# Two sums moved ahead of an addition, and a looser wait for their transfers, in a Strassen MLP

## The chip, the cores and the metric

The kernel runs on one core of one Trainium2 chip. The metric is device time in microseconds, 1420.25 us for the kernel before (median of 3 runs, 1419.57 to 1420.36). A core has TensorE for matrix products, VectorE, ScalarE and GpSimd for elementwise work, and SyncE, which here only issues transfers. Each engine works through its own list of instructions in order; they meet at semaphores. TensorE writes to eight banks of PSUM, everything else lives in SBUF.

## The reference

Two transformer blocks in float32 on 512 tokens of width 1024 (the second with 16 more). The attention parts are of no matter here. Each block ends in an MLP with a squared ReLU:

```
x = x + jnp.square(jax.nn.relu(h2 @ w_mlp_in[layer])) @ w_mlp_out[layer]      # first block
hdn = jnp.square(jax.nn.relu(jnp.einsum('bld,df->blf', u, w_ff1)))            # second block
return jnp.einsum('blf,fd->bld', hdn, w_ff2)
```

The hidden width is 4096.

## The kernel before

Every float32 product is made of three: each operand is split into a high part (the float32 rounded to the matmul's own format, written by ScalarE) and a low part (the rest, a subtraction on VectorE), and TensorE adds high x high, high x low and low x high in PSUM. So every weight passes ScalarE and then VectorE before TensorE may use it.

An MLP takes its hidden width in four chunks of 1024. The first three of each MLP run in a hardware loop over `strassen_chunk`, six chunks in all; the fourth is dense. In a chunk, eight slabs (j = 0 to 7) make the hidden values with dense products at L2120. The second matrix is then applied in four column pairs (q = 0 to 3) of 256 output columns, each as a 2 x 2 block product in the Strassen-Winograd form, with 7 products (128 output columns, 512 of k, 256 tokens) instead of 8. One such product is `block_product` at L2168: 4 blocks of k times 3 matmuls of 256 columns, 12 in all, so 84 a pair and 336 a chunk. Its order in a pair is A11 B11, S1 T1, S2 T2, S3 T3, S4 B22, A12 B21, A22 T4. S1 to S4 are sums of quarters of the weights, T1 to T4 differences of quarters of the hidden values.

Who makes what:

- S1 and S3 come from transfers that GpSimd issues in `s13_sums`: first two plain ones (the base, L738), and when these have landed two that accumulate onto them (L741). There are two buffers, pair q and pair q+2 share one.
- S2 and S4 are VectorE's `second_sum` (L1390: S1 plus a quarter of the weights that SyncE loaded) and `fourth_sum` (L1396). ScalarE writes their high parts (L896, in pair 0 L888 and L892), VectorE the low ones: `last_low` (L1418), and for pair 0 `second_low` (L1410) and `fourth_low` (L1414). S4's low part gives the semaphore s4_lo.
- `upper_left` (L1400) and `first_sums` (L1405) are the low parts of A11 and of S1 with S3; `lower` (L1423) those of A12 and A22.
- PSUM is used in two sets of four banks, one for odd and one for even pairs. In a pair the partial sums of two banks are needed in `mids` as well as in the output. VectorE adds them there twice: `first_mids` (L1432) after the first two products, and L1494 after S2 and S3. Both give mid_read. TensorE waits for the first before S4 B22 and for the second before A22 T4, since those products go on adding in banks that VectorE has to read first.
- At the end of a pair VectorE adds to X at L1503 and L1507.
- For the last hidden slab (j = 7) the differences T2 and T4 are still being split while pair 0 runs: L1473 is the low part of T2, L1478 that of T4. TensorE waits for them by k, through `ready` and `all_ready`.

The order on every engine is the order in which this code is written; no scheduler changes it.

Of the kernel before, what the change touches and what calls it, by code (L numbers as in the profile page):

```python
# [47 lines left out]
B11, T1, T2_, T3, T4, B21, B22 = range(7)  # L48
# [123 lines left out]
def build(nc, d):  # L172
# [21 lines left out]
    with ctx:  # L194
# [165 lines left out]
        s2_hi, s2_lo, s4_hi, s4_lo = sem("s2_hi"), sem("s2_lo"), sem("s4_hi"), sem("s4_lo")  # L360
# [299 lines left out]
        def _(pool):  # L660
# [64 lines left out]
            def s13_sums(which, c, q):  # L725
# [7 lines left out]
                if u > 1:  # L733
                    pool.wait_ge(s13_lo, u - 1)
                    pool.wait_ge(s2_sum, u - 1)
                for o, s in ((0, S3), (1, S1_)):
# [565 lines left out]
        def _(dve):  # L1302
# [69 lines left out]
            def strassen_chunk(which, c):  # L1372
# [62 lines left out]
                for j in range(8):  # L1435
# [24 lines left out]
                    else:  # L1460
# [7 lines left out]
                        if j == 6:  # L1468
                            upper_left(0)
                        if j == 7:  # L1470
                            first_mids(0)
                        dve.wait_ge(hid_hi, parts + 4 + 2 * k + 1)
                        dve.tensor_tensor(hidden_part(Hl, k, T2_, 2), h[:, 0:2].rearrange("p b n -> p (b n)"),  # L1473
                                          hidden_part(Hh, k, T2_, 2), ALU.subtract).then_inc(hid_lo, 1)
                        if j == 7:
                            fourth_low(0)
                        dve.wait_ge(hid_hi, parts + 4 + 2 * k + 2)
                        dve.tensor_tensor(hidden_part(Hl, k, T4, 3), h[:, 2:5].rearrange("p b n -> p (b n)"),  # L1478
# [6 lines left out]
                for q in range(4):  # L1485
# [4 lines left out]
                    if q > 0:  # L1490
                        first_mids(q)
                    dve.wait_ge(blk_done, done + 4)
                    dve.wait_ge(mid_read, reads + 2 * q + 1)
                    dve.tensor_tensor(mid, mid, ps[:, g2:g4 + 1, 0:HB], ALU.add).then_inc(mid_read, 1)  # L1494
                    if last:
                        slab_weights(p0, 0, t + 17)
                    else:
                        upper_left(q + 1)
                        second_sum(q + 1)
                        fourth_sum(q + 1)  # L1500
                        first_sums(q + 1)
# [601 lines left out]
        def _(pe):  # L2103
# [49 lines left out]
            def strassen_chunk(which, c):  # L2153
# [8 lines left out]

                def block_product(a, b, bank, first, ready=None, ks=range(4)):
                    for k in ks:
                        if ready is not None:
# [11 lines left out]
                for q in range(4):  # L2177
# [18 lines left out]
                    else:  # L2196
                        pe.wait_ge(s4_lo, pairs + q + 1)
                    block_product(S2_, T2_, g2, True, ready, range(3))
                    block_product(S3_, T3, g4, True, None, range(3))
                    block_product(S2_, T2_, g2, True, ready, range(3, 4)).then_inc(blk_done, 1)  # L2200
                    block_product(S3_, T3, g4, True, None, range(3, 4)).then_inc(blk_done, 1)
                    pe.wait_ge(s4_lo, pairs + q + 1)
# [500 lines left out]
```

## Time and profile before

| what | value |
|---|---|
| median of 3 runs | 1420.25 us |
| the profiled execution's own time | 1420.25 us |
| its span | 1418.5 us |
| TensorE busy | 1410.9 us, 99% |
| VectorE busy | 898.3 us, 63% |
| ScalarE busy | 578.8 us, 41% |
| GpSimd busy | 197.6 us, 14% |
| share of the chain of waits at the dense products, L2120 | 65% |
| share at the block products, L2168 | 17% |

The span runs from the first to the last instruction that the profile holds; the time of the execution has 1.75 us more around it. A busy share tells how full an engine is, not what an instruction waits for; for that the views by wait and by time are needed. "PE" is TensorE's matmuls and "PEld" its weight loads, which overlap them; DVE is VectorE, ACT ScalarE, POOL GpSimd, SP SyncE.

### The profile page before, as it was taken

The numbers are of one execution on the slowest core, as the hardware profiler recorded it, in microseconds if no ns is written. First come the engines' busy times: TensorE is split into PE (matmuls) and PEld (weight loads), VectorE is DVE, ScalarE is ACT, GpSimd is POOL, SyncE is SP. The second block draws the span as 40 slices with busy tenths as digits, with TensorE's granted clock in tenths as the row PEclk, the third lists the DMA queues.
The fourth block names the chain that finished last, engine by engine and source line by source line (L and its number), as shares of the span: only waits on it lengthen the run. The fifth ranks groups of instructions, "written<-read, shape, count | busy, mean of one in ns | idle before, by whom it ended". The sixth has DMA issues, their size and how long they took to land.

```text
span 1418.5 us, 21381 instructions
## 1 busy us (share of the span) xinstructions
PE 1410.9 (99%) x8574; PEld 1183.2 (83%) x8574; DVE 898.3 (63%) x1200; ACT 578.8 (41%) x828; POOL 197.6 (14%) x204
## 2 busy tenths in 40 slices
PE   9999999999999999999999999999999999999998
PEld 7887778777888989989878997778888998989886
DVE  5535433665757858577656778656756858668652
ACT  4124531554445435353244435343344535344232
POOL 4000000000022302211322020000022211302300
PEclk9999999999999999999999999999999999999999
DMA  5223113201236745635323222232236663836321
GB/s 182 89 90 111 61 61 108 70 30 60 98 108 164 183 131 147 159 109 148 102 77 104 90 68 76 83 99 74 92 105 157 160 166 101 202 111 178 109 84 60
DMA packets 154715, 156.35 MB, mean 110 GB/s; under 512 B 3866, under 2 KB 148612, under 8 KB 154644
## 3 DMA queue, kind: packets, MB, share of 16 engines
q1 hardware_dynamic: 125444, 130.16, 28.8%
q0 software_dynamic: 29184, 25.17, 10.0%
q8 instruction: 52, 0.85, 0.3%
q14 instruction: 19, 0.16, 0.0%
q10 hardware_dynamic: 16, 0.00, 0.0%
HBM read 152.44 MB, written 2.10 MB: 109 GB/s over the span
## 4 chain that ended last, share of the span: by engine, by line
PE 98%; DVE 1%; ACT 1%; issue 0%; POOL 0%; POOLq 0%; DVEq 0%
PE ps L2120 65%; PE ps L2168 17%; PE ps L2116 4%; PE ps L2237 3%; PE ps L2466 1%; PE ps L2493 1%; PE ps L2479 1%; PE ps L2582 1%; DVE wl L1313 1%; PE ps L2285 0%; PE ps L2370 0%; PE ps L2277 0%; PE ps L2346 0%; PE ps L2411 0%; PE ps L2390 0%; PE ps L2262 0%
## 5 line engine op out<-in xcount | busy, mean ns | idle before, releaser
L2120 PE MATMUL ps<-AA,wh 128*128 128x512 f32 x1600 | 505.3, 397 | 0.4
L2120 PEld LDWEIGHTS ps<-AA,wh 128*128 128x128 f32 x1600 | 296.7, 188 | 71.8 <-DVE wl L1313 2.9
L2120 PE MATMUL ps<-BB,wh 128*128 128x512 f32 x1088 | 342.5, 396 | 0.2 <-issue 0.2
L2120 PE MATMUL ps<-AA,wl 128*128 128x512 f32 x800 | 314.9, 394 | 0.0
L2120 PEld LDWEIGHTS ps<-BB,wh 128*128 128x128 f32 x1088 | 202.2, 188 | 49.7 <-issue 1.9
L829 ACT ACTIVATE wh<-raw 128x1024 fp32r<-128x1024 f32 (+2 forms) x149 | 141.5, 950 | 233.4 <-PE ps L2120 222.4
L2120 PE MATMUL ps<-BB,wl 128*128 128x512 f32 x544 | 213.9, 393 | 0.0
L1313 DVE TENSOR_TENSOR wl<-raw,wh 128x1024 fp32r<-128x1024 f32 (+2 forms) x149 | 174.9, 1174 | 49.4 <-ACT wh L829 49.0
L2120 PEld LDWEIGHTS ps<-AA,wl 128*128 128x128 f32 x800 | 150.5, 188 | 34.2
L2120 PEld LDWEIGHTS ps<-BB,wl 128*128 128x128 f32 x544 | 102.3, 188 | 23.2
L2168 PE MATMUL ps<-Hl,wh 128*128 128x256 f32 x384 | 108.7, 283 | 0.0
L1349 DVE TENSOR_TENSOR arena<-ps,RS 128x512 f32<-128x512 f32 (+2 forms) x59 | 40.8, 691 | 88.2 <-PE ps L2120 82.9
L2168 PE MATMUL ps<-Hl,Sh 128*128 128x256 f32 x288 | 80.9, 281 | 0.0
L1381 DVE TENSOR_TENSOR wl<-raw,wh 128x1024 fp32r<-128x1024 f32 x48 | 62.3, 1297 | 28.8 <-ACT wh L875 13.7
L2168 PEld LDWEIGHTS ps<-Hl,wh 128*128 128x128 f32 x384 | 73.3, 191 | 0.0
L875 ACT ACTIVATE wh<-raw 128x1024 fp32r<-128x1024 f32 x36 | 38.3, 1063 | 70.3 <-PE ps L2120 70.1
L1443 DVE SCALAR_TENSOR_TENSOR zf<-ps,RS 128x512 f32<-128x512 f32 x48 | 33.2, 691 | 47.8 <-PE ps L2120 47.2
L2168 PEld LDWEIGHTS ps<-Hl,Sh 128*128 128x128 f32 x288 | 54.6, 190 | 0.3
L2168 PE MATMUL ps<-AA,wh 128*128 128x256 f32 x192 | 54.2, 282 | 0.0
L2168 PE MATMUL ps<-BB,wh 128*128 128x256 f32 x192 | 54.2, 282 | 0.0
L2168 PE MATMUL ps<-AA,wl 128*128 128x256 f32 x192 | 53.7, 280 | 0.0
L2168 PE MATMUL ps<-BB,wl 128*128 128x256 f32 x192 | 53.7, 280 | 0.0
(331 smaller groups left out, 2185.2 us busy)
## 6 DMA issues: line engine op xcount, KB each, us to landing
raw<-in_w_in SPq DMA_DIRECT2D x38, 1024.0 KB, 5.5
raw<-in_w_ff SPq DMA_DIRECT2D x29, 1024.0 KB, 5.5
raw<-in_w_mlp_in SPq DMA_DIRECT2D x16, 1024.0 KB, 5.4
raw<-in_w_mlp_out SPq DMA_DIRECT2D x16, 1024.0 KB, 5.3
zf<-in_w_mlp_out POOLq DMA_DIRECT2D x48, 256.0 KB, 4.4
zf<-in_w_ff POOLq DMA_DIRECT2D x48, 256.0 KB, 4.3
raw<-in_w_out SPq DMA_DIRECT2D x8, 1024.0 KB, 5.2
late<-in_w_ff SPq DMA_DIRECT2D x3, 1024.0 KB, 5.4
```

The costliest lines, as they stand in the source:

```text
L829: act.activation(w_slab(wh, t % 2, kt), raw_slab(t), ACT.Copy).then_inc(hi_ready, 1)
L875: act.activation(w_slab(wh, j % 2, KT), raw_half((p0 + i) % 2, j % 2, KT, 2), ACT.Copy)\
L1313: dve.tensor_tensor(w_slab(wl, t % 2, kt), raw_slab(t), w_slab(wh, t % 2, kt), ALU.subtract)\
L1349: dve.tensor_tensor(tokens(dst, kind), dense_psum(t, kind)[0:rows], tokens(scale, kind), ALU.mult)\
L1381: dve.tensor_tensor(w_slab(wl, slot, KT), raw_half(p % 2, slot, KT, 2), w_slab(wh, slot, KT), ALU.subtract).then_inc(lo_ready, 1)
L1443: dve.scalar_tensor_tensor(out=f, in0=halves(dense_psum(t0 + j, which)), scalar=0.0, in1=halves(RS[:, 0:S1]), op0=ALU.max, op1=ALU.mult).t ...
L2116: last = pe.matmul(dense_psum(t_ps, ALL)[:, half, :], a[:, k, :], b[:, o0 + k, half * HALF2:(half + 1) * HALF2], start=start, stop=stop)
L2120: last = pe.matmul(dense_psum(t_ps, kind), a[:, k, :], b[:, o0 + k, col0:col0 + S1], start=start, stop=stop)
L2168: mm = pe.matmul(ps[:, bank, 0:HB], w[:, k, :], hidden_part(x, k, b), start=(first and k == 0 and i == 0), stop=(k == 3 and i == 2), skip_ ...
L2237: mm = pe.matmul(out, x[:, k, tok], w[:, k, cols], start=False, stop=(k == KT - 1 and i == 2), skip_group_check=True)
L2466: pe.matmul(ps[:, 2 + b, 0:nk], qb[rows, hp, n * P:(n + 1) * P], kb[rows, hp, 0:nk], start=True, stop=False)
L2479: mm = pe.transpose(ps[:, 4 + b, i * P:(i + 1) * P], pair(Sg[w % 2], nk)[:, b, i * P:(i + 1) * P], ident[:, :])
```

## The change

There are three edits, all in the Strassen chunks. GpSimd's transfers for the sums of pair q wait for s4_lo of pair q-2 in place of two other semaphores of that pair. VectorE runs `first_mids(0)` behind `fourth_low(0)`, and `second_sum(q + 1)` and `fourth_sum(q + 1)` ahead of the second addition to `mids` in pair q. TensorE runs all of S2 T2 and then all of S3 T3, where before their fourth k came behind the first three of both.

```diff
--- before.py
+++ after.py
@@ -731,8 +731,7 @@
                 if c == 0 and q == 0:
                     pool.wait_ge(slab_done, MLPS[which][0] + 1)
                 if u > 1:
-                    pool.wait_ge(s13_lo, u - 1)
-                    pool.wait_ge(s2_sum, u - 1)
+                    pool.wait_ge(s4_lo, u - 1)
                 for o, s in ((0, S3), (1, S1_)):
                     at = slice(q * 256 + o * P, q * 256 + o * P + P)
                     pool.dma_start(blk(sums[:, s]), rows[0:S1, at].rearrange("(k p) n -> p k n", p=P))                        .then_inc(s13_base, 16)
@@ -1467,13 +1466,12 @@
                                                  op0=ALU.mult, op1=ALU.subtract).then_inc(t4_diff, 1)
                         if j == 6:
                             upper_left(0)
-                        if j == 7:
-                            first_mids(0)
                         dve.wait_ge(hid_hi, parts + 4 + 2 * k + 1)
                         dve.tensor_tensor(hidden_part(Hl, k, T2_, 2), h[:, 0:2].rearrange("p b n -> p (b n)"),
                                           hidden_part(Hh, k, T2_, 2), ALU.subtract).then_inc(hid_lo, 1)
                         if j == 7:
                             fourth_low(0)
+                            first_mids(0)
                         dve.wait_ge(hid_hi, parts + 4 + 2 * k + 2)
                         dve.tensor_tensor(hidden_part(Hl, k, T4, 3), h[:, 2:5].rearrange("p b n -> p (b n)"),
                                           hidden_part(Hh, k, T4, 3), ALU.subtract).then_inc(hid_lo, 1)
@@ -1489,6 +1487,9 @@
                     mid = halves(mids[:, q])
                     if q > 0:
                         first_mids(q)
+                    if not last:
+                        second_sum(q + 1)
+                        fourth_sum(q + 1)
                     dve.wait_ge(blk_done, done + 4)
                     dve.wait_ge(mid_read, reads + 2 * q + 1)
                     dve.tensor_tensor(mid, mid, ps[:, g2:g4 + 1, 0:HB], ALU.add).then_inc(mid_read, 1)
@@ -1496,8 +1497,6 @@
                         slab_weights(p0, 0, t + 17)
                     else:
                         upper_left(q + 1)
-                        second_sum(q + 1)
-                        fourth_sum(q + 1)
                         first_sums(q + 1)
                     dve.wait_ge(blk_done, done + 6)
                     dve.tensor_tensor(halves(x0), halves(x0), ps[:, g1:g3 + 1, 0:HB], ALU.add)
@@ -2160,8 +2159,8 @@
                 S4_, S2_ = (blk(wh[:, 0, upper]), blk(wl[:, 0, upper])), (blk(wh[:, 0, lower]), blk(wl[:, 0, lower]))
                 A11_, S3_, S1_ = ((blk(Sh[:, i * S1:(i + 1) * S1]), blk(Sl[:, i * S1:(i + 1) * S1])) for i in range(3))
 
-                def block_product(a, b, bank, first, ready=None, ks=range(4)):
-                    for k in ks:
+                def block_product(a, b, bank, first, ready=None):
+                    for k in range(4):
                         if ready is not None:
                             ready(k)
                         for i, (w, x) in enumerate(((a[0], Hh), (a[0], Hl), (a[1], Hh))):
@@ -2195,10 +2194,8 @@
                             pe.wait_ge(hid_lo, parts + 4 + 2 * k + 2)
                     else:
                         pe.wait_ge(s4_lo, pairs + q + 1)
-                    block_product(S2_, T2_, g2, True, ready, range(3))
-                    block_product(S3_, T3, g4, True, None, range(3))
-                    block_product(S2_, T2_, g2, True, ready, range(3, 4)).then_inc(blk_done, 1)
-                    block_product(S3_, T3, g4, True, None, range(3, 4)).then_inc(blk_done, 1)
+                    block_product(S2_, T2_, g2, True, ready).then_inc(blk_done, 1)
+                    block_product(S3_, T3, g4, True).then_inc(blk_done, 1)
                     pe.wait_ge(s4_lo, pairs + q + 1)
                     pe.wait_ge(mid_read, reads + 2 * q + 1)
                     block_product(S4_, B22, g3, False, all_ready).then_inc(blk_done, 1)
```

What this moves on TensorE, in pair 0 of a chunk. Weights in `wh` and `wl` are S2's, those in `Sh` and `Sl` are S3's; the wait for hid_lo is for one k of T2's low part. Before, from the third k of S3 to its fourth, with the fourth k of S2 between them:

```order
L2168 MATMUL ps<-AA,Sh 128x256
L2168 MATMUL ps<-Hl,Sh 128x256
L2168 MATMUL ps<-AA,Sl 128x256
L2193 REGISTER_ALU
L2168 MATMUL ps<-AA,wh 128x256 [waits hid_lo]
L2168 MATMUL ps<-Hl,wh 128x256
L2168 MATMUL ps<-AA,wl 128x256
L2168 MATMUL ps<-AA,Sh 128x256
L2168 MATMUL ps<-Hl,Sh 128x256
L2168 MATMUL ps<-AA,Sl 128x256
```

and now the third and the fourth k of S2, with S3 from there on:

```order
L2167 MATMUL ps<-AA,wh 128x256 [waits hid_lo]
L2167 MATMUL ps<-Hl,wh 128x256
L2167 MATMUL ps<-AA,wl 128x256
L2192 REGISTER_ALU
L2167 MATMUL ps<-AA,wh 128x256 [waits hid_lo]
L2167 MATMUL ps<-Hl,wh 128x256
L2167 MATMUL ps<-AA,wl 128x256
L2167 MATMUL ps<-AA,Sh 128x256
L2167 MATMUL ps<-Hl,Sh 128x256
L2167 MATMUL ps<-AA,Sl 128x256
L2167 MATMUL ps<-AA,Sh 128x256
```

The wait for the fourth k of T2's low part comes nine matmuls earlier, and the matmuls are the same.

On VectorE in pair 0, from `first_mids(0)` (L1432) to `upper_left(1)` (L1400), before:

```order
L1432 TENSOR_TENSOR zf<-zf,ps 128x512
L1472 REGISTER_ALU
L1473 TENSOR_TENSOR Hl<-zf,AA 128x512
L1414 TENSOR_TENSOR wl<-zf,wh 128x512
L1477 REGISTER_ALU
L1478 TENSOR_TENSOR Hl<-zf,AA 128x768
L1422 REGISTER_ALU
L1423 TENSOR_TENSOR wl<-raw,wh 128x1024
L1492 REGISTER_ALU
L1494 TENSOR_TENSOR zf<-zf,ps 128x512
L1399 REGISTER_ALU
L1400 TENSOR_TENSOR Sl<-raw,Sh 128x512
```

and now, from `fourth_low(0)` (L1413) to the second addition to `mids` (L1495); the low part of T2 (L1470) stands directly ahead of the first row. Line numbers are those of the changed kernel:

```order
L1413 TENSOR_TENSOR wl<-zf,wh 128x512
L1430 ISA
L1431 TENSOR_TENSOR zf<-zf,ps 128x512
L1475 REGISTER_ALU
L1476 TENSOR_TENSOR Hl<-zf,AA 128x768
L1421 REGISTER_ALU
L1422 TENSOR_TENSOR wl<-raw,wh 128x1024
L1389 TENSOR_TENSOR zf<-zf,raw 128x512
L1394 REGISTER_ALU
L1395 TENSOR_TENSOR zf<-raw,zf 128x512
L1493 REGISTER_ALU
L1495 TENSOR_TENSOR zf<-zf,ps 128x512
```

`first_mids(0)` (now L1431) has moved behind the low parts of T2 and S4, and the two sums (now L1389 and L1395) stand ahead of the second addition, where before they came behind it and behind `upper_left(1)`.

On GpSimd, the transfers of pair 2 of the first chunk and the beginning of pair 3, before:

```order
L738 DMA zf<-in_w_mlp_out 128x4x128 [waits s2_sum,s13_lo]
L738 DMA zf<-in_w_mlp_out 128x4x128
L741 DMA zf<-in_w_mlp_out 128x4x128 [waits s13_base]
L741 DMA zf<-in_w_mlp_out 128x4x128
L738 DMA zf<-in_w_mlp_out 128x4x128 [waits s2_sum,s13_lo]
```

and now:

```order
L737 DMA zf<-in_w_mlp_out 128x4x128 [waits s4_lo]
L737 DMA zf<-in_w_mlp_out 128x4x128
L740 DMA zf<-in_w_mlp_out 128x4x128 [waits s13_base]
L740 DMA zf<-in_w_mlp_out 128x4x128
L737 DMA zf<-in_w_mlp_out 128x4x128 [waits s4_lo]
```

The transfers stand where they stood; only what the first of each pair waits for has changed.

## Rows read from the trace of the kernel before

**Rows 1.** Busy time of the engines, and the granted clock by slice, from the page.
```profile
PE 1410.9 (99%) x8574; PEld 1183.2 (83%) x8574; DVE 898.3 (63%) x1200; ACT 578.8 (41%) x828; POOL 197.6 (14%) x204
...
PEclk9999999999999999999999999999999999999999
```

**Rows 2.** Chain of waits in order of time: start us, us, engine, line, count.
```profile
462.27 39.90 PE ps L2168 x336
502.17 44.48 PE ps L2120 x192
```

**Rows 3.** Waits: engine and line <- releaser: us in total, times, longest us.
```profile
PE ps L2277 <- POOL ident L671: 1.7, 1, 1.7
...
DVE zf L1494 <- PE ps L2168: 33.9, 18, 2.1
```

**Rows 4.** Timeline: start us, us, engine, line, operation; TensorE in pair 0.
```profile
465.87 0.19 PEld L2168 LDWEIGHTS ps<-AA,Sh 128*128 128x128 f32 x1
...
470.53 0.19 PEld L2168 LDWEIGHTS ps<-AA,wh 128*128 128x128 f32 x1
470.64 0.28 PE L2168 MATMUL ps<-AA,wh 128*128 128x256 f32 x1
```

**Rows 5.** Timeline, VectorE in pair 0.
```profile
465.13 0.69 DVE L1432 TENSOR_TENSOR zf<-zf,ps 128x512 f32<-128x512 f32 x1 [0.21 <-PE ps L2168]
465.74 0.68 DVE L1473 TENSOR_TENSOR Hl<-zf,AA 128x512 fp32r<-128x512 f32 x1
...
467.81 1.22 DVE L1423 TENSOR_TENSOR wl<-raw,wh 128x1024 fp32r<-128x1024 f32 x1
468.94 0.68 DVE L1494 TENSOR_TENSOR zf<-zf,ps 128x512 f32<-128x512 f32 x1
...
470.14 0.69 DVE L1390 TENSOR_TENSOR zf<-zf,raw 128x512 f32<-128x512 f32 x1
470.94 0.69 DVE L1396 TENSOR_TENSOR zf<-raw,zf 128x512 f32<-128x512 f32 x1
471.54 1.22 DVE L1405 TENSOR_TENSOR Sl<-zf,Sh 128x1024 fp32r<-128x1024 f32 x1
...
473.28 1.22 DVE L1418 TENSOR_TENSOR wl<-zf,wh 128x1024 fp32r<-128x1024 f32 x1
```

**Rows 6.** Timeline, ScalarE in pair 0.
```profile
464.50 0.63 ACT L920 ACTIVATE AA<-zf 128x512 fp32r<-128x512 f32 x1 [0.83 <-DVE zf L1464]
465.03 0.62 ACT L892 ACTIVATE wh<-zf 128x512 fp32r<-128x512 f32 x1
```

**Rows 7.** Timeline, a stall of TensorE on a dense slab of the second block.
```profile
741.70 2.03 DVE L1313 TENSOR_TENSOR wl<-raw,wh 128x1024 fp32r<-128x1024 f32 x1 [0.20 <-ACT wh L829]
...
743.79 0.30 PEld L2120 LDWEIGHTS ps<-AA,wh 128*128 128x128 f32 x2 [0.58 <-DVE wl L1313]
...
744.12 0.19 PEld L2120 LDWEIGHTS ps<-AA,wl 128*128 128x128 f32 x1
```

**Rows 8.** Timeline, VectorE in pair 1.
```profile
477.94 0.69 DVE L1494 TENSOR_TENSOR zf<-zf,ps 128x512 f32<-128x512 f32 x1 [1.37 <-PE ps L2168]
```

**Rows 9.** Timeline, transfers issued by GpSimd for the sums, and one by SyncE.
```profile
430.30 2.60 POOL L738 DMA_DIRECT2D zf<-in_w_mlp_out  x2
440.32 2.63 POOL L741 DMA_DIRECT2D zf<-in_w_mlp_out  x2 [7.42 <-DMA zf<-in_w_mlp_out]
457.74 1.54 POOL L738 DMA_DIRECT2D zf<-in_w_mlp_out  x2 [14.79 <-DVE zf L1390]
...
469.19 0.37 SPq L609 DMA_DIRECT2D raw<-in_w_mlp_out  x1
...
473.06 1.55 POOL L738 DMA_DIRECT2D zf<-in_w_mlp_out  x2 [8.18 <-DVE Sl L1405]
477.77 2.62 POOL L741 DMA_DIRECT2D zf<-in_w_mlp_out  x2 [3.17 <-DMA zf<-in_w_mlp_out]
```

**Rows 10.** DMA issues of 478.77 to 479.37: kind, KB each, us to landing.
```profile
zf<-in_w_mlp_out POOLq DMA_DIRECT2D x2, 256.0 KB, 5.8
```

## The prediction

> **What bounds the kernel now.** I read the page first. TensorE is busy 1410.9 of 1418.5 us [rows 1], so a change can gain only where TensorE waits, and costs only where it makes TensorE wait. The chain of waits then shows where the changed code stands: the four column pairs of one chunk are one unbroken piece of 336 matmuls in 39.90 us [rows 2], and there are six such pieces (three chunks in each of two MLPs). That is 0.1188 us a matmul and 9.97 us a pair. The list of waits has TensorE wait 1.7 us once, at the start of the program, and nowhere at the line of the block products [rows 3]. So nothing in the changed stretch can be won by taking a wait away. The question is whether the new order brings a producer behind TensorE. For that I lay the timeline of TensorE beside those of VectorE, ScalarE and GpSimd in the first of the six pieces and compare each semaphore that TensorE waits for with the time at which TensorE gets there. The other five pieces repeat it.
>
> TensorE's marks in pair 0 [rows 4]: the 34th of its 84 weight loads at 465.87; the last product (A22, the 73rd to 84th matmul) loads weights at 470.53 and multiplies from 470.64. Counted on from there, pair 1 starts at 470.64 + 12 x 0.1188 = 472.07, and its own A22 at 470.64 + 9.97 = 480.61.
>
> **The change part by part.**
>
> *Order of the products S2 and S3 on TensorE.* The same 24 matmuls are issued, twelve and twelve instead of 9, 9, 3, 3. The last of them ends at the same place, and nobody waits for the signal of S2 alone. The piece runs at one pitch, switches of product included, so I cost the order itself at 0 (bound: the last rival, 0.03 us a switch). What moves is one wait: in pair 0 the fourth k of S2 needs the low part of T2_ (VectorE L1473), and now needs it at the 34th weight load, 465.87, instead of nine matmuls later (466.94). In its old place, at 465.74 behind `first_mids` [rows 5], L1473 would be late by 0.5 us. In the new order it comes ahead of `first_mids` and waits only for ScalarE's L920, which ends at 464.50 + 0.63 = 465.13 [rows 6]. A waiting engine starts about 0.06 us after its releaser's end [rows 7], so L1473 runs about from 465.18 to 465.87: a tie. If it is lost, it costs 0.0 to 0.1 us, and it does not add to what follows, since the term below is set by VectorE alone.
>
> *`first_mids(0)` behind `fourth_low(0)`.* From L1432 to L1494 VectorE runs without a gap, 465.13 to 468.94 = 3.81 us [rows 5]. It is the same five instructions in another order, all their inputs are there (ScalarE's L892 for `fourth_low` ends at 465.65 [rows 6]). The run starts at 465.18, so the first instruction behind it starts at 468.99. `first_mids` itself ends 1.2 us later than before, at 467.06 by three instructions of 0.60 us; TensorE's S4 product wants it 24 loads ahead of 470.53, at about 467.7. Hidden, with 0.6 us in hand.
>
> *`second_sum(q+1)` and `fourth_sum(q+1)` ahead of the second addition to `mids`.* This is the term that I think decides. TensorE may not start A22 of pair q, which goes on writing the same bank, until the second addition to `mids` (L1494) has read it. Before, in pair 0, L1494 ran 468.94 to 469.62, 0.9 us before TensorE's weight load at 470.53 [rows 4, 5]. Now two sums stand ahead of it. Their pitches are read from the same place: L1390 at 470.14, L1396 at 470.94, the next at 471.54, that is 0.80 + 0.60 = 1.40 us [rows 5]. So L1494 starts at 468.99 + 1.40 = 470.39 and ends at 470.39 + 0.68 = 471.07. TensorE needed it 0.5 us earlier.
>
> What such a wait costs is seen at a stall on a dense slab. VectorE ends at 741.70 + 2.03 = 743.73, the weight load starts at 743.79 and the third one at 744.12 [rows 7]. In a running stream a load starts with the matmul ahead of its own, and the pitch there is 44.48 / 192 = 0.23 us [rows 2]; so the third load marks the second matmul, and the first ran from 743.89, 0.16 us after VectorE's end. Here that gives 471.07 + 0.16 = 471.23 against 470.64: **0.59 us lost in pair 0 of each chunk**. Behind it TensorE is again the only bound, so it stays lost: 6 x 0.59 = 3.5 us.
>
> The cover in the other pairs: in pair 1 VectorE stood idle 1.37 us, until the S3 product was done, before L1494 at 477.94 [rows 8], so from 476.57. The two sums fill that gap, and L1494 has until about 479.8. In the pairs behind it the gap is up to 2.1 us [rows 3]. Hidden, as long as the sums' data have landed. The rest of VectorE's order in pair 0 ends where it ended: L1405 started at 471.54, and now at 468.99 + 1.40 + 0.60 + 0.60 = 471.59; L1418 behind it ends at 474.55 (before 474.50) for a wait of TensorE 24 matmuls into pair 1, at about 474.8, which itself moves 0.59 us later. L1400, now behind L1494, ends at 470.39 + 0.60 + 0.69 = 471.68 for the first product of pair 1 at 472.07 + 0.59. Each of these is hidden.
>
> *GpSimd's wait.* The transfers that build the sums of pair q+2 now start behind the low part of S4 of pair q instead of behind the second sum and the low parts of S1 and S3. For pair 2 this is a delay from 457.74 [rows 9] to about 466.8: `fourth_low(0)` ends at 465.18 + 0.60 + 0.69 = 466.47, and GpSimd issued 0.30 us after its releaser's end at 473.06 (471.54 + 1.22 = 472.76) [rows 5, 9]. From there the fitting row is the transfers of pair 3, which also share the DMA engines with a 1 MB load of SyncE: 473.06 to 477.77 for the base, 1.3 us to the second accumulating issue, 5.8 us to its landing [rows 9, 10], 11.8 us in all. So pair 2's sums land at 466.77 + 11.84 = 478.6, and `second_sum(2)` starts at 478.7. VectorE then stands 2.1 us on this wait (from 476.57), with L1494 queued behind it. L1494 then ends at 478.67 + 1.40 + 0.68 = 480.75, and A22 of pair 1 starts at 480.91 instead of 480.61: 0.3 us late. But pair 0 has already put TensorE back by 0.59, so this second lateness lies inside the first and adds nothing: per chunk the larger of the two counts. It starts to add when `second_sum(2)` begins after 478.96. Bounds: at the least the transfers cost nothing (with `second_sum(2)` at 478.37 they would be in time even alone). At the most they take what pair 1's took in the first chunk, 430.30 to 440.32 for the base alone [rows 9], 5.3 us more: a loss of 5.6 us in pair 1 instead of 0.59 in pair 0, 34 us in all. I take the 11.8 us, because that slow case was issued right behind the accumulating transfers of pair 0, while at 466.8 GpSimd's queue has long been empty. Pair 3's transfers now start behind L1418 at about 474.9 (before 473.06) and land at 486.7; TensorE needs them by about 488.9. Those of the next chunk's pairs 0 and 1 start 0.5 to 2 us later than before with over 20 us in hand.
>
> A rule of the skill speaks the other way. The Trainium skill ("DMA: Bandwidth & Descriptors", section "Anatomy of one DMA — SWDGE (gpsimd) path") fits a GpSimd-issued transfer as 2.0 us plus its bytes at 436 GB/s, 2.6 us for 256 KB. By it the sums would land at about 474.1 and GpSimd's wait would cost nothing at all. This case's trace does not agree for accumulating transfers, 5.8 us [rows 10], so the trace decides; the forecast is the same by either.
>
> **Sum.** Added 6 x 0.59 = 3.5 us; removed 0. The profiled execution took 1420.25 us, 1.75 around its span of 1418.5, and that is also the median of the runs. Forecast 1423.8 us, +0.25%. A measurement of this kernel tells about 0.2% (2.8 us) from no change.
>
> **Rivals.**
>
> *The weights are already in.* If the blocked product's weight load need not wait, the first matmul starts at 471.07 + 0.06 and the loss is 0.49 us, 2.9 us in all: 1423.2. For it: loads run 0.11 us ahead of their matmuls here [rows 4]. Against it: the one stall that is seen has its load behind the wait [rows 7], though there it waited for the weights themselves. The Trainium skill ("TensorE: Matmul & The Clock Gate", step "LDWEIGHTS — get the stationary operand into the array") says that the queue pulls weight loads ahead of matmuls in flight; by that rule the time would be this one. No row here shows it across a wait.
>
> *TensorE catches up.* The pitch of 118.8 ns for 256 columns [rows 2] is 0.464 ns a column, that of 231.7 ns for 512 columns 0.453, at the upper of the clock's two levels throughout [rows 1]; so at least 2.9 ns of a block product's matmul is not columns. If that surplus is issue time, the queue fills during a stall, and the 264 matmuls from there to the end of the piece could give 0.59 us back: 1420.3, no slower than before. It decides from 2.2 ns of recovery a matmul. Against it: the 192 matmuls of a dense stretch and the 336 of a piece each keep one pitch [rows 2], with SyncE, VectorE and ScalarE coming and going beside them, and no stretch is seen to run faster. Likewise, if L1494's read came in time after all, the time would be this one.
>
> *The sums land late.* Pair 2's transfers start 2.4 us before SyncE's load at 469.19 [rows 9], and pair 3's meet theirs at another point, so the sharing may be worse. At 1 us later than I say, `second_sum(2)` begins at 479.7, pair 1 loses 1.3 us instead of 0.59, and the kernel 7.8 us: 1428.
>
> *The new order itself is faster.* Two switches of product fewer per pair; at 0.03 us each, 48 of them give 1.4 us, with no stall 1418.8. No pitch in the trace shows such a cost.
>
> **How the numbers follow.** Forecast (0.59 us a chunk) 0.58; weights already in 0.12; catching up or in time 0.13; late sums 0.14; faster order 0.03. The likeliest one's own range is 1423.0 to 1424.6. The range of 8 in 10 leaves out the catching up below and the worse half of the late sums: 1421.5 to 1427.0. Faster by over 0.2%: 0.03. Within 0.2%: the catching up, a third of the case with weights in, and a few hundredths of the forecast's lower edge, 0.20. Slower: 0.77.
>
> **What would show it.** Right: the waits list a new one of TensorE at the block products for L1494 (now L1495), six times, near 0.5 us each; each piece of 336 matmuls takes 40.5 us instead of 39.90; VectorE waits for a DMA ahead of `second_sum(2)` and GpSimd's wait there names L1413. The forecast is wrong if pair 0 shows no gap at A22, if the gap stands at pair 1 and exceeds 0.6 us (late sums), or if the pieces still take 39.9 us.

## The result, and the profile after

| | us, median (lowest to highest, runs) | ratio to before, 95% interval |
|---|---|---|
| before | 1420.25 (1419.57 to 1420.41, 5) | |
| changed | 1428.4 (1424.97 to 1431.81, 5) | 1.0061 [1.0041, 1.0082] |

The kernel became slower, by 8 us, where I forecast 3.5 us. The time of 1428.4 us lies outside my range of 1421.5 to 1427.0. It also spreads over 7 us from run to run, where the kernel before kept within 0.9. The profiled execution of the changed kernel took 1423.29 us (span 1421.6), less than all five timed ones, so its trace shows the fixed part of the loss well and the rest only at its smallest.

The chain of waits after (start us, us, engine and line, count) answers to [rows 2]. Line 2119 is the dense products and 2167 the block products.

```profile
420.09 41.72 PE ps L2119 x180
...
470.56 31.38 PE ps L2167 x264
501.94 44.49 PE ps L2119 x192
...
1302.06 0.78 POOL zf L740
1302.84 7.05 DMA zf<-in_w_ff
1310.01 0.70 DVE zf L1389
1311.34 0.69 DVE zf L1495
1312.08 11.58 PE ps L2167 x96
1323.66 44.49 PE ps L2119 x192
```

The first piece began at 420.09 + 41.72 = 461.81 and ended at 501.94: 40.13 us instead of 39.90. It is no longer one link: the chain enters it at 470.56, the A22 product of pair 0. The last piece is entered much later, at 1312.08, by way of a transfer that took 7.05 us. The six pieces took 40.13, 40.22, 40.13, 40.69, 40.12 and 41.49 us.

The waits (engine and line <- releaser: us in total, times, longest us) answer to [rows 3]. L1495 is the second addition to `mids`, L1389 `second_sum`, L1413 the low part of S4, L737 GpSimd's base transfers.

```profile
DVE zf L1389 <- DMA zf<-in_w_ff: 12.7, 6, 3.9
DVE zf L1495 <- PE ps L2167: 12.4, 6, 2.2
DVE zf L1389 <- DMA zf<-in_w_mlp_out: 12.0, 6, 2.6
...
PE ps L2167 <- DVE zf L1495: 2.6, 8, 1.1
```

Three of these are new. VectorE waits for a DMA ahead of `second_sum` twelve times: six are pair 2, as forecast, and six are pair 3, which I had in time. TensorE waits for L1495 eight times, not six: in pair 0 of each chunk, once in pair 1 (0.36 us, in the fourth chunk) and once in pair 2 (1.28 us, in the sixth).

Pair 0 on VectorE and TensorE (timeline: start us, us, engine, line, operation) answers to [rows 4, 5]; this execution runs 0.47 us ahead of the one before.

```profile
464.68 0.69 DVE L1470 TENSOR_TENSOR Hl<-zf,AA 128x512 fp32r<-128x512 f32 x1 [0.24 <-ACT AA L919]
...
468.50 0.68 DVE L1389 TENSOR_TENSOR zf<-zf,raw 128x512 f32<-128x512 f32 x1
469.21 0.69 DVE L1395 TENSOR_TENSOR zf<-raw,zf 128x512 f32<-128x512 f32 x1
469.82 0.68 DVE L1495 TENSOR_TENSOR zf<-zf,ps 128x512 f32<-128x512 f32 x1
...
478.36 0.69 DVE L1389 TENSOR_TENSOR zf<-zf,raw 128x512 f32<-128x512 f32 x1 [2.32 <-DMA zf<-in_w_mlp_out]
```

```profile
469.93 0.19 PEld L2167 LDWEIGHTS ps<-AA,wl 128*128 128x128 f32 x1
470.56 0.19 PEld L2167 LDWEIGHTS ps<-AA,wh 128*128 128x128 f32 x1 [0.43 <-DVE zf L1495]
```

VectorE's run came as forecast. L1495 ends at 470.50, the weight load follows 0.06 us behind, and it comes 0.63 instead of 0.12 us after the load ahead of it. Counted from the start of the piece it comes at 470.56 - 461.81 = 8.75 us, where it came at 470.53 - 462.27 = 8.26 us [rows 2, 4].

GpSimd's issues for the sums in the same chunk, and SyncE's single loads of 1 MB, answer to [rows 9]:

```profile
466.28 1.55 POOL L737 DMA_DIRECT2D zf<-in_w_mlp_out  x2 [23.97 <-DVE wl L1413]
471.54 2.61 POOL L740 DMA_DIRECT2D zf<-in_w_mlp_out  x2 [3.71 <-DMA zf<-in_w_mlp_out]
474.27 1.55 POOL L737 DMA_DIRECT2D zf<-in_w_mlp_out  x2
481.48 2.62 POOL L740 DMA_DIRECT2D zf<-in_w_mlp_out  x2 [5.66 <-DMA zf<-in_w_mlp_out]
...
475.60 0.37 SPq L609 DMA_DIRECT2D raw<-in_w_mlp_out  x1
...
485.49 0.37 SPq L609 DMA_DIRECT2D raw<-in_w_mlp_in  x1
```

The third line is the one to look at. Pair 3's base transfers (474.27) are issued with no idle time behind pair 2's accumulating ones, and SyncE's load follows 1.3 us later. From this base to its accumulating issue it is 7.2 us here, where I had 4.7.

### The profile page after: what moved, and what is told of

It reads as the page before. It is cut to its first block, busy times and chain, and to the rows that moved or that the text cites. A ratio compares the mean times of both kernels' runs of the same rounds, so it can differ in the third digit from the quotient of the medians.

```text
span 1421.6 us, 21342 instructions
## 1 busy us (share of the span) xinstructions
PE 1411.4 (99%) x8574; PEld 1182.0 (83%) x8574; DVE 897.9 (63%) x1200; ACT 579.1 (41%) x828; POOL 198.8 (14%) x204
## 4 chain that ended last, share of the span: by engine, by line
PE 92%; DVE 3%; DMA 2%; issue 1%; ACT 1%; POOL 0%; DVEq 0%; POOLq 0%
PE ps L2119 65%; PE ps L2167 11%; PE ps L2115 4%; PE ps L2234 3%; DMA zf<-in_w_ff 2%; PE ps L2463 1%; PE ps L2282 1%; PE ps L2490 1%; PE ps L2476 1%; PE ps L2579 1%; DVE wl L1312 0%; DVE wl L1422 0%; DVE zf L1495 0%; PE ps L2367 0%; DVE zf L1389 0%
```

## The experiments

Every time below is a median beside runs of the kernel before on the same chip (1419.66 to 1420.0 us). "Fixed part" is what every execution loses, "late sums" what varies.

### The change again, and without its transfer wait

`again` is the changed kernel. `oldwait` gives GpSimd its old wait back:

```diff
-                    pool.wait_ge(s4_lo, u - 1)
+                    pool.wait_ge(s13_lo, u - 1)
+                    pool.wait_ge(s2_sum, u - 1)
```

`newwait` is the kernel before with that one edit the other way round. `q1up` is the changed kernel in which pair 0 keeps its sums behind the second addition to `mids`.

> The changed kernel once more, for a second trace and more times. Late-sums theory (the sums of pairs 2 and 3 land so close to the point where VectorE needs them that each execution loses a different amount): the times scatter again, 1424 to 1432, and the trace shows VectorE waiting for a DMA at second_sum before pairs 2 and 3, with TensorE's waits at the block products longer in some chunks. Rival (a fixed loss in the order of the instructions): all times within 1 us of each other.

> The changed kernel with GpSimd's two old waits (s13_lo and s2_sum of the pair two before). Late-sums theory: the scatter goes, and what is left is the fixed loss in pair 0, where the two sums stand ahead of the second addition: 6 x 0.24 to 6 x 0.59, so 1421.7 to 1423.8, all runs within 1 us. Rival 1 (the scatter comes from VectorE's or TensorE's new order): still 1425 to 1432. Rival 2 (the loss in pair 0 is made up by TensorE in full): 1420.3.

> The kernel before with the one edit on GpSimd's wait (s4_lo). Late-sums theory: pair 2's sums are wanted at 17 us into the piece instead of 14.5, so most landings are in time, but the transfers still pile up: scatter stays in part, median 1421 to 1426. If the wait costs only together with the sums' earlier place on VectorE: 1420.3. Rival 1 (VectorE's order is the cause): 1420.3 and no scatter.

> The changed kernel, but in pair 0 of each chunk the two sums stand again behind the second addition; in pairs 1 and 2 they stay ahead of it. Fixed-loss theory: the gap of TensorE at A22 in pair 0 is gone, and the kernel is 1.4 us (6 x 0.24) to 3.5 us (6 x 0.59) faster than the changed one, or less where late sums in pair 1 now show that had been hidden behind it. The late sums stay: median 1424 to 1428, and scatter.

Measured: `again` 1432.33 us (1427.49 to 1435.03), ratio 1.0087 [1.0074, 1.01]. `oldwait` 1422.42 (1421.21 to 1422.82), 1.0019 [1.001, 1.0027]. `newwait` 1429.5 (1420.37 to 1436.39), 1.0058 [1.0035, 1.0081]. `q1up` 1431.32 (1421.45 to 1440.25), 1.0075 [1.005, 1.01].

So the spread and the larger part of the loss go with GpSimd's wait: it is there in the three kernels that have the new wait and gone in the one that has not. I had it too small: `newwait` and `q1up` lie above what I expected of them (1421 to 1426 and 1424 to 1428), so the wait does harm with the sums in their old place too. `q1up` can't be told from `again` within that spread, so it says nothing on the fixed part.

In the profiled execution of `again` the late sums are plain. VectorE in pairs 2 and 3 of the first chunk:

```profile
478.48 0.69 DVE L1389 TENSOR_TENSOR zf<-zf,raw 128x512 f32<-128x512 f32 x1 [2.70 <-DMA zf<-in_w_mlp_out]
...
493.64 0.69 DVE L1389 TENSOR_TENSOR zf<-zf,raw 128x512 f32<-128x512 f32 x1 [7.62 <-DMA zf<-in_w_mlp_out]
```

GpSimd's issues that led there, and TensorE at the A22 product that waits for L1495 behind them:

```profile
472.02 2.61 POOL L740 DMA_DIRECT2D zf<-in_w_mlp_out  x2 [4.47 <-DMA zf<-in_w_mlp_out]
474.01 2.17 POOL L737 DMA_DIRECT2D zf<-in_w_mlp_out  x2
484.13 2.62 POOL L740 DMA_DIRECT2D zf<-in_w_mlp_out  x2 [7.95 <-DMA zf<-in_w_mlp_out]
```

```profile
495.71 0.29 PEld L2167 LDWEIGHTS ps<-AA,wh 128*128 128x128 f32 x1 [5.20 <-DVE zf L1495]
495.88 0.34 PEld L2167 LDWEIGHTS ps<-Hl,wh 128*128 128x128 f32 x1
```

From the base to the accumulating issue it was 484.13 - 474.01 = 10.1 us, as long as the slow case of [rows 9], and pair 3's sums landed at 493.6 instead of my 486.7. TensorE stood 5.2 us, and what followed ran slowly. The same execution by stretches (busy time of each engine, granted clock, DMA share):

```profile
488.50:492.00 3.50, 2.21 (x19) 2.01 (x18) 0.00 (x0) 0.00 (x0) 0.00 (x0) 1.00 1.10 291
492.00:495.50 3.50, 0.00 (x0) 0.00 (x0) 1.83 (x3) 1.40 (x2) 0.06 (x1) 0.60 0.74 187
495.70:499.50 3.80, 3.79 (x17) 3.79 (x18) 3.76 (x5) 1.27 (x2) 2.41 (x3) 0.50 0.60 73
499.50:503.00 3.50, 3.50 (x31) 3.50 (x31) 1.91 (x2) 0.30 (x1) 1.48 (x2) 0.99 1.04 208
```

During the stall the granted clock fell from 1.00 to 0.50 (from 2.4 to 1.2 GHz) and stayed there for the first 3.8 us of work, 17 matmuls instead of some 32. The 96 matmuls from 495.71 took 13.36 us by the chain, against 96 x 0.1188 = 11.4. The low clock added 2 us to a stall of 5. TensorE stood idle when it fell, and was at work again when it rose.

### Which pair's wait

`only2` and `not2` are the kernel before with the new wait for pair 2 alone, and for all pairs but pair 2. `serial` is `newwait` with one wait more, so that a pair's base is never issued over the accumulating transfers of the pair ahead. `order` is the kernel before with the new order of S2 and S3 and the new place of `first_mids(0)` alone.

```diff
+                    if q == 2:                      # only2; not2 has q != 2
+                        pool.wait_ge(s4_lo, u - 1)
+                    else:
                         pool.wait_ge(s13_lo, u - 1)
                         pool.wait_ge(s2_sum, u - 1)
```

```diff
+                    pool.wait_ge(s4_lo, u - 1)      # serial
+                    pool.wait_ge(s13_sum[(u - 1) % 2], 32 * ((u - 1) // 2) + 32)
```

> The kernel before with GpSimd's new wait for pair 2 alone (the other pairs keep the two old ones). Pile-up theory (the loss comes when pair 3's base transfers are issued while pair 2's accumulating ones are in flight): pair 2 starts at 5 us into the piece and accumulates until 17, pair 3's base is issued at 11, inside it; so the scatter and a median of 1423 to 1432, as in the kernel with the wait changed for all pairs. Rival (each pair's own later start is what costs, pair 3's most): little loss, 1420 to 1421.

> The kernel before with GpSimd's new wait for pairs 0, 1 and 3 and the two old ones for pair 2. Pile-up theory: pair 2's sums have landed before pair 3's base is issued, 1.8 us later than before; no loss and no scatter, 1419.7. Rival (own later start of pair 3): a loss of 1 to 10 us with scatter.

> The kernel before with GpSimd's new wait, and a further one: the base of a pair is issued only when the accumulating transfers of the pair ahead have landed. Pile-up theory: without the overlap each pair takes 11 to 12 us from issue to landing instead of up to 19, so although pair 3 is issued 4 us later still (at about 478.6), it lands at about 490.3; VectorE wants it at 489, so TensorE loses 0 to 1 us a chunk and the times lie close together, 1420 to 1424. Rival (later start costs by itself): worse than without the further wait, above 1430.

> The kernel before with the two remaining edits alone: TensorE's order of S2 and S3, and first_mids(0) behind fourth_low(0). Both theories: 1419.7 within 0.3 us; at most 6 x 0.1 us more if the low part of T2 comes late for its fourth k in the new place. Rival (the order itself is worth something): over 1 us away on either side.

Measured: `only2` 1428.95 us (1420.0 to 1434.61), ratio 1.0051 [1.0032, 1.0071]. `not2` 1420.08 (1418.99 to 1420.49), 1.0001 [0.9992, 1.001]. `serial` 1457.5 (1456.21 to 1461.08), 1.0268 [1.0255, 1.0282]. `order` 1419.3 (1418.84 to 1419.93), 0.9996 [0.9987, 1.0004].

The late sums come through pair 2's wait alone, though it is pair 3 that is late. Pair 3 itself has the old wait in `only2` and the new one in `not2`, and its base starts at nearly the same time, 474.18 and 474.63. What differs is what it finds when it starts. In `not2` pair 2 was issued at 457.58 and 462.25 and was out of the way, and pair 3's base was back in 5.7 us; in `only2` it took 10.0.

`serial` missed by 35 us, and that ends the simple form of my theory, that only the overlap with the pair ahead does harm. Its rival, that a later start costs by itself, had the right side (above 1430). GpSimd in its first chunk:

```profile
480.34 1.54 POOL L738 DMA_DIRECT2D zf<-in_w_mlp_out  x2 [5.73 <-DMA zf<-in_w_mlp_out]
485.01 2.62 POOL L741 DMA_DIRECT2D zf<-in_w_mlp_out  x2 [3.13 <-DMA zf<-in_w_mlp_out]
```

The base is back at 485.01 - 480.34 = 4.7 us. But it starts six microseconds later, and now the accumulating pair meets SyncE's load of 485.8: VectorE got its data only at 494.5, 9.5 us behind the issue. So there are two ways to be late here: a slow base, and a start six microseconds later.

### What stretches the landing

In `light_first` the first 1 MB load of a chunk (485.5) brings 128 KB, in `light_last` the last one (475.6); each is the changed kernel otherwise, and the rest of that slab keeps old numbers.

```diff
+                        ks = slice(0, 1 if i == 0 else KT)   # light_first; light_last has i == 7
-                        sp.dma_start(raw[:, (p0 + i) % 2, :].rearrange("p (k n) -> p k n", k=KT),
-                                     src.rearrange("(k p) n -> p k n", p=P))\
+                        sp.dma_start(raw[:, (p0 + i) % 2, :].rearrange("p (k n) -> p k n", k=KT)[:, ks, :],
+                                     src.rearrange("(k p) n -> p k n", p=P)[:, ks, :])\
```

> The changed kernel, but the first weight load of every chunk of the two Strassen layers (raw, 1 MB, issued by SyncE at 485.5 in the traces of the changed kernel) brings 128 KB instead of 1 MB; the rest of that slab keeps old numbers, so the output is another. Theory A: what stretches the landing of pair 2's and pair 3's accumulating transfers (from 5 to 10 us) is the weight load that shares the 16 DMA engines with them. The transfers of pair 3 (issued 481.5 to 484.1) then land by 489.5 at the latest, VectorE no longer waits for the DMA ahead of pair 3's sums (2.2 to 7.6 us before), the wait before pair 2 (for transfers of 471.5 to 478) stays at 2.3 to 2.7 us, and the spread of 7 us between executions goes: 1422.4 +/- 1 us. Theory B: the transfers of GpSimd hold each other up, with no part of the load: pair 3's sums are late as before, 1428 to 1432 us with the same spread.

> The changed kernel, but the last weight load of every chunk (raw, 1 MB, issued at 475.6) brings 128 KB; output another. Theory A (sharing with the weight loads): pair 2's accumulating transfers (issued 471.5) land before 477, VectorE's wait of 2.3 to 2.7 us before pair 2 is under 1 us; pair 3's base transfers (474.3) land in 4 to 5 us, so its accumulating ones are issued at 479 to 480 instead of 481.5 to 484, and land before the load of 485.5 is under way: no wait before pair 3, 1422.4 +/- 1 us. Theory B: base to accumulating issue stays 7 to 10 us, 1428 to 1432 us.

Measured: `light_first` 1424.51 us (1423.78 to 1427.44), ratio 1.0032 [1.002, 1.0045]. `light_last` 1422.37 (1422.03 to 1422.83), 1.0019 [1.001, 1.0028], which is `oldwait`'s time, with no spread. The DMA issues around 476 (KB each, median us to landing), in `again` and then in `light_last`. They are SyncE's load and pair 3's base, both of its transfers in `again` and the second one in `light_last`, where both together give 5.1:

```profile
raw<-in_w_mlp_out SPq DMA_DIRECT2D x1, 1024.0 KB, 9.5
zf<-in_w_mlp_out POOLq DMA_DIRECT2D x2, 256.0 KB, 8.0
```

```profile
zf<-in_w_mlp_out POOLq DMA_DIRECT2D x1, 256.0 KB, 5.2
raw<-in_w_mlp_out SPq DMA_DIRECT2D x1, 128.0 KB, 4.8
```

And VectorE at pair 3 in `light_last`, then in `light_first` (its execution of 1427.44 us, the slowest of six; the others took 1423.8 to 1425.2):

```profile
486.81 0.69 DVE L1390 TENSOR_TENSOR zf<-zf,raw 128x512 f32<-128x512 f32 x1 [0.84 <-DMA zf<-in_w_mlp_out]
```

```profile
491.38 0.69 DVE L1390 TENSOR_TENSOR zf<-zf,raw 128x512 f32<-128x512 f32 x1 [5.23 <-DMA zf<-in_w_mlp_out]
```

With the load of 475.6 cut to an eighth, pair 3's sums are there at 486.8, what I had forecast for the full loads (486.7), and the time is down by 6 to 10 us. With the load of 485.5 cut instead, they still come at 491.4. So the load at 475.6 has a part in it, as theory A says, and the other one a smaller part: the spread shrinks and the median falls by 4 to 8 us, but its forecast of no wait failed. In `light_last` too I had VectorE's waits too small: in the first chunk it stood 2.08 us ahead of pair 2's sums (forecast under 1) and 0.84 ahead of pair 3's (forecast none). TensorE didn't feel it; it waits in the six pairs 0 alone. Theory B, that GpSimd's transfers hold each other up with no part of the loads, falls with `light_last`.

But the load is not enough by itself. In `after_not2`, a run of the next section in which pair 2 is out of the way, pair 3's base starts at the same time as in the changed kernel, ahead of the same full load. GpSimd there, and then in `light_last`:

```profile
474.29 1.55 POOL L741 DMA_DIRECT2D zf<-in_w_mlp_out  x2 [9.79 <-DVE wl L1421]
479.08 2.62 POOL L744 DMA_DIRECT2D zf<-in_w_mlp_out  x2 [3.25 <-DMA zf<-in_w_mlp_out]
```

```profile
474.46 1.84 POOL L738 DMA_DIRECT2D zf<-in_w_mlp_out  x2
480.75 2.62 POOL L741 DMA_DIRECT2D zf<-in_w_mlp_out  x2 [4.44 <-DMA zf<-in_w_mlp_out]
```

From base to accumulating issue it is 4.8 us with the load alone, 6.3 with pair 2's accumulating transfers ahead and the load cut, and 7.2 to 10.1 with both. It takes the two together. Each of these is the first chunk of one execution.

### The fixed part

All four have old waits for pair 2 at least. `q1up_old` is `q1up` with old waits. `three_ahead` is `oldwait` with one more VectorE instruction of 0.60 us ahead of L1495 in pair 0, a dose. `sums` is the kernel before with only the two sums moved ahead in pairs 0 to 2. `after_not2` is the changed kernel with the old wait for pair 2 alone.

```diff
-                    if not last:                    # q1up, q1up_old
+                    if not last and q > 0:
                         second_sum(q + 1)
                         fourth_sum(q + 1)
...
+                    if q == 0:                      # three_ahead
+                        upper_left(1)
```

> The changed kernel with the waits of GpSimd's transfers as before, and with pair 0 keeping its sums behind the second addition to mids; pairs 1 and 2 have them ahead. My theory: all of the fixed loss lies in pair 0, so this one is back at the order-only kernel, 1419.3 to 1420.3 us, ratio under 1.0004, and the gap of 0.43 us in TensorE before A22 of pair 0 is gone. Rival (the loss is spread over pairs): 1421 to 1422.4 us.

> The changed kernel with the old waits of GpSimd's transfers, and in pair 0 one more VectorE instruction of 0.60 us (upper_left of pair 1) ahead of the second addition to mids, so that A22's weight load is 1.0 to 1.1 us late instead of 0.43. Theory C (a delay of VectorE is paid in full by TensorE behind it): 6 chunks x 0.60 = 3.6 us more than the kernel with the two sums ahead, 1426.0 us, ratio 1.0044. Rival (TensorE makes half of it up in its next products): 1.8 us more, 1424.2 us. Rival (made up in full): 1422.4 us.

> The kernel before with one edit: second_sum and fourth_sum stand ahead of the second addition to mids in pairs 0 to 2 (old order of S2 and S3, old place of first_mids(0), old waits). My theory: this edit holds all of the fixed loss: the kernel with pair 0 left as it was is at 1418.1, this one 6 chunks x 0.46 to 0.59 us above the order's 1419.3 to 1420.3, so 1421.5 to 1423.5 us, ratio 1.0010 to 1.0025. Rival (the fixed loss needs first_mids(0) behind fourth_low too, which puts VectorE later): under 1420.5 us. TensorE waits 0.4 us at pair 0's A22 in each of 6 chunks by my theory, for under 0.15 us by the rival.

> The changed kernel with the old wait of GpSimd's transfers for pair 2 alone (the others keep the new one). My theory: late transfers come only through pair 2, whose base transfers start 8.7 us later under the new wait and push pair 3's into SyncE's 1 MB load of 475.6; with pair 2 back at its place this one is the kernel with all old waits, 1421.2 to 1422.8 us, ratio 1.0019, with no spread and no wait of VectorE for the DMA. Rival (with the sums moved ahead, the waits of pairs 0, 1 and 3 cost too): over 1424 us, spread over some us.

| | us, median (lowest to highest) | ratio, 95% interval | six pieces and what lies between, us |
|---|---|---|---|
| before | | | 858.34 |
| order | 1419.3 (1418.84 to 1419.93) | 0.9996 [0.9987, 1.0004] | 857.50 |
| q1up_old | 1418.1 (1417.66 to 1418.96) | 0.9988 [0.9979, 0.9997] | 857.54 |
| sums | 1421.19 (1420.75 to 1422.41) | 1.0011 [1.0002, 1.002] | 860.48 |
| after_not2 | 1421.93 (1421.45 to 1422.57) | 1.0016 [1.0007, 1.0026] | 860.47 |
| oldwait | 1422.42 (1421.21 to 1422.82) | 1.0019 [1.001, 1.0027] | 860.74 |
| three_ahead | 1425.29 (1425.08 to 1425.5) | 1.0038 [1.0025, 1.0052] | 864.15 |
| changed | 1428.4 (1424.97 to 1431.81) | 1.0061 [1.0041, 1.0082] | 861.85 (its execution of 1423.29 us) |

The last column runs from the start of the first piece to the end of the last, by the chain of each profiled execution (before: 1320.61 - 462.27). It leaves out what differs between executions ahead of this stage.

Leaving pair 0 as it was takes the whole fixed part away: `q1up_old` has 857.54, `order`'s 857.50. Against it `oldwait` has 3.2 us more, 0.53 us a chunk. A further 0.60 us of VectorE ahead of L1495 costs 864.15 - 860.74 = 3.4 us, 0.57 a chunk: paid nearly in full (by the medians of the two kernels it is 2.9 us). The wait itself is steadier than these averages. From the start of a piece A22's weight load comes at 8.25 us in `order` and `q1up_old`, at 8.75 in `sums` and `oldwait` and at 9.36 in `three_ahead`, in the first piece of either MLP within 0.02: 0.50 us for the two sums and 0.61 more for the dose. `after_not2` shows in the changed kernel itself that pair 2's wait accounts for the late sums; VectorE's waits for a DMA ahead of its sums are down to three, 1.1 us at most. `sums` shows that the moved sums alone make the wait, 0.4 us at A22 of each pair 0, without the later `first_mids(0)`; the waits of `sums` and of `oldwait`:

```profile
PEld ps L2169 <- DVE zf L1497: 2.5, 6, 0.4
```

```profile
PEld ps L2168 <- DVE zf L1496: 2.7, 6, 0.5
```

The kernel `order` gained something that I had at 0; it holds two edits, the new order of the products and the new place of `first_mids(0)`, and no run parts them. The chain of `order` (a piece of the first MLP, then one of the second):

```profile
462.29 39.62 PE ps L2167 x336
...
1111.18 39.88 PE ps L2167 x336
```

The three pieces of the first MLP take 39.62 us instead of 39.90, those of the second 39.88. In the kernel before products of twelve matmuls take 1.41 or 1.44 us, and in the first piece of `order` fewer of them take 1.44. The same two paces show behind every stall of pair 0: the last 264 matmuls take 31.37 or 31.60 us, in `oldwait`, `sums` and `three_ahead` alike. They aren't made by the stall, since `order` has both with none (39.62 - 8.24 = 31.38 and 39.88 - 8.26 = 31.62). What puts a piece in the one or the other pace I did not settle; it is worth 0.25 us a piece. It hides part of the loss in the changed kernel's own trace: the four pieces without late sums are 0.22 to 0.32 us longer than 39.90, though each has its stall of 0.5. It also makes the edits not add up: `sums` alone lost 2.1 us and `order` alone gained 0.8, together they lose 2.4.

`q1up_old` is the best version found, 1418.1 us, and its interval lies below 1. At 0.12% the gain is smaller than what one comparison of this kernel can be trusted for, and its stage is no shorter than `order`'s.

## Why the prediction was wrong, step by step

- *The bound, and that only a late producer can matter*: right. TensorE is busy 1409 to 1416 us in all but one of these kernels, and every loss is a wait of it, or the low clock behind one.
- *Order of S2 and S3 at 0*: nearly. The tie at T2_'s low part was lost by some 0.03 us (VectorE's L1470 ends at 465.37, the weight load follows at 465.43), and A22 came no later for it in `order`. But `order` gained 0.8 us over the stage, a small part of what my rival of the faster order wanted. I had ruled any effect out because the trace kept one pitch; the single products, which I did not read, had two.
- *`first_mids(0)` hidden*: right.
- *0.59 us in pair 0*: the mechanism and the place are right, and the size is near. A22's load came 0.50 us later. Over the stage of `oldwait` it was 0.53 us a chunk against `q1up_old`, and 0.40 against before, since the better pace hides a part. The two sums took 469.82 - 468.50 = 1.32 us ahead of L1495, not the 1.40 of [rows 5], which is most of the difference. As a sum: 3.5 us forecast, 3.2 - 0.8 = 2.4 measured over the stage.
- *The weights are already in*: this rival falls, by its mechanism and not by its time, which was only 0.6 us from the forecast's. The load itself waited for VectorE, 470.50 to 470.56. The Trainium skill ("TensorE: Matmul & The Clock Gate", step "LDWEIGHTS — get the stationary operand into the array") has the queue pull loads ahead of matmuls in flight; here a load did not pass a semaphore wait of its own product.
- *TensorE catches up*: it falls too. `three_ahead` pays 95% of its dose over the stage, and the quicker of the two paces is there in `order` without any stall to make good.
- *GpSimd's wait for pair 2*: `second_sum(2)` was forecast for 478.7 and began at 478.36; with the 0.47 us by which this execution runs ahead added, 478.83. In `again` (0.74 us ahead) it was 479.2, past the 478.96 from which I had it add, and TensorE lost 0.29 us there; in the fourth chunk of the changed kernel's first trace it lost 0.36. So this part was right in its size, but with nothing in hand.
- **The step that failed is the next sentence of it**: "Pair 3's transfers now start behind L1418 at about 474.9 and land at 486.7; TensorE needs them by about 488.9." They started at 474.0 to 474.3 and landed at 488.1 in the mild execution and at 493.6 in `again`. I had priced the slow case, 430.30 to 440.32 for a base issued right behind accumulating transfers [rows 9], and set it aside because GpSimd's queue is empty at 466.8. That holds for pair 2. But delaying pair 2 puts its accumulating transfers at 471.5 to 474.2, directly ahead of pair 3's base: the slow case's own condition, moved one pair on. And at 475.6 SyncE's load comes down on both, with the next one at 485.5. The slow case had that neighbour too, a 1 MB load that SyncE issued at 431.66, 1.4 us behind the base. I moved one transfer and did not lay the queue out again behind it. That the base takes 4.8 us from the same start when pair 2 is out of the way (`after_not2`), and 7.2 to 10.1 when it is not, shows this step to be the one.
- *Late sums*: this is the rival that came true, at 0.14, with the right sign and 1428 us for its time (1428.4). That the time fits so well is luck; my range ended at 1427.0 because it left out the worse half of this case. Its place was wrong in the main: I had it at pair 2 and TensorE's pair 1, where TensorE loses 0.2 to 0.4 us in some chunks; the large losses are at pair 3 and TensorE's pair 2. And it is no fixed microsecond: the six pieces of `again` took 47.5, 40.6, 40.4, 40.8, 40.1 and 40.4 us in its profiled execution of 1430.02 us, so the excess is one chunk's for the most part.
- The rule of the Trainium skill ("DMA: Bandwidth & Descriptors", section "Anatomy of one DMA — SWDGE (gpsimd) path"), 2.6 us for 256 KB, comes out short here. It is a rule for one transfer, and these run in pairs; taken as one of 512 KB, a pair would come to 3.2 us by it, an estimate. Each of a base pair took 3.6 us in the kernel before and 3.9 in the changed one (466.28), an accumulating one 5.6, and the base behind accumulating transfers and beside the 1 MB load 8.0 (`again`).

## What to carry to other kernels

When an edit delays a transfer, write down the whole queue of the DMA engines behind it, with every other engine's loads, and read the price of each transfer from a row with the same neighbours; the delayed one may be in time and the one behind it late. Where a kernel's runs begin to spread, look for a transfer that lands near its deadline. A trace that is fast by chance shows such a fault only at its edge, so count the waits and not only the time.

## What the runs showed of the hardware

- In a stall of TensorE of 5.2 us (`again`) the granted clock fell from 1.00 to 0.50, and it came back 3.8 us after work began: 2 us more. Stalls of 0.3 to 1.3 us left it at 1.00, and so did one of 2.5 us in `light_first`. One of 2.3 us in `q1up` had 1.00 to its end at 584.19, but at 585.1, with TensorE at work again, the clock fell to 0.50, and it came back at 588.5.
- The two 256 KB base transfers of pair 3, issued behind pair 2's accumulating ones, landed in 5.1 us (median) beside a 128 KB load, and beside a 1 MB one in 5.5 us in the first trace of the changed kernel and 8.0 in `again`. That load itself took 8.2 and 9.5 us, against 5.2 in the kernel before. Why the time differs so much between executions with the same issue times is open.
- A base pair issued right behind accumulating transfers and followed by a 1 MB load took 7.2, 9.0 (`light_first`) and 10.1 us to the issue that waits for it, and 6.3 with the load cut. With the load and nothing of GpSimd's ahead it took 4.8 (`after_not2`) and 5.7 (`not2`), and 4.7 where it started 3.1 us ahead of the load (the kernel before). I did not run a kernel in which the accumulating transfers are plain ones, so how much is due to accumulating as such is not shown.
- TensorE runs the block products at one of two paces, 31.37 or 31.60 us for the last 264 matmuls of a piece, behind a stall of pair 0 or with none, at a granted clock of 1.00.
